# First norm of an encoder layer: statistics per token on tokens-major x, gain and split taken from PSUM, small loads behind the first weights

## What is computed

```python
def rmsnorm(x, g):
    xf = x.astype(jnp.float32)
    y = xf * lax.rsqrt(jnp.mean(xf * xf, axis=-1, keepdims=True) + EPS)
    return (y * g.astype(jnp.float32)).astype(x.dtype)

def hybrid_mixer(h, w_in, ...):          # h = rmsnorm(x, norm_mix)
    (qkv_a, a_pre, b_pre, z_a, q_b, k_b, v_b, i_b, f_b, o_b,
     q_c, k_c, v_c, gate_pre) = _split_cols(h @ w_in, IN_SIZES)
...
x = x + hybrid_mixer(rmsnorm(x, norm_mix[l]), w_in[l], ...)
```

## Time and profile before

| | |
|---|---|
| median of 3 runs | 2091.82 us (2091.56 to 2091.86) |
| the profiled execution | 2091.85 us |
| its span, first to last instruction | 2089.7 us |
| mean granted TensorE clock | 0.993 of full speed |
| busy: PE / DVE / ACT / POOL | 2045.9 / 1229.5 / 895.5 / 34.0 us |
| moved by DMA | 377.44 MB, 181 GB/s on average |

### The profile page before, as it was taken

How to read it: one execution, slowest core, us unless ns; L and a number is a source line. 1 busy time by engine, 2 the same in 40 slices (tenths; PEclk the granted TensorE clock), 3 DMA queues, 4 the chain that set the end, 5 groups by cost and what they waited for, 6 DMA issues and landing times.

```text
span 2089.7 us, 36639 instructions
## 1 busy us (share of the span) xinstructions
PE 2045.9 (98%) x15803; PEld 1974.7 (94%) x15803; DVE 1229.5 (59%) x1312; ACT 895.5 (43%) x864; POOL 34.0 (2%) x44
## 2 busy tenths in 40 slices
PE   5999999999999999999999999999999999999998
PEld 5999999999999999999999999888888888899998
DVE  5477644543544557577474445677877777744443
ACT  4444433344446434355444434544444444433332
POOL 2000000000000000000000000000000000000000
PEclk8999999999999999999999999999999999999999
DMA  7555444366455865655565355656655655566663
GB/s 220 162 184 185 137 135 133 109 207 198 150 177 176 297 203 177 226 162 181 182 196 167 122 160 171 223 173 199 193 179 190 201 181 180 180 202 198 185 195 126
DMA packets 358512, 377.44 MB, mean 181 GB/s; under 512 B 11913, under 2 KB 354723, under 8 KB 357123
## 3 DMA queue, kind: packets, MB, share of 16 engines
q1 hardware_dynamic: 354771, 353.36, 53.3%
q0 software_dynamic: 3632, 22.42, 2.9%
HBM read 364.75 MB, written 11.01 MB: 180 GB/s over the span
## 4 chain that ended last, share of the span: by engine, by line
PE 94%; DVE 3%; ACT 2%; issue 1%; DMA 0%; POOL 0%; SPq 0%; DVEq 0%; ACTq 0%
PE bank L1700 21%; PE bank L1702 21%; PE bank L1701 21%; PE bank L1734 15%; PE bank L1736 8%; PE bank L1911 1%; DVE w_lo L973 1%; PE bank L1858 1%; ACT w_hi L456 1%; PE bank L2114 1%; PE bank L2095 1%; DVE tmp L1017 1%; DVE x_home L1023 0%; PE bank L1845 0%; PE bank L1777 0%
## 5 line engine op out<-in xcount | busy, mean ns | idle before, releaser
L973 DVE TENSOR_TENSOR w_lo<-raw,w_hi 128x2048 fp32r<-128x2048 f32 (+1 forms) x352 | 763.6, 2169 | 624.4 <-ACT w_hi L456 624.0
L456 ACT ACTIVATE w_hi<-raw 128x2048 fp32r<-128x2048 f32 (+1 forms) x354 | 644.1, 1820 | 1098.7 <-PE bank L1702 823.8
L1700 PE MATMUL bank<-x_home,w_hi 128*128 128x256 f32 x2304 | 650.5, 282 | 18.8 <-DVE x_home L1023 15.4
L1701 PE MATMUL bank<-x_home,w_hi 128*128 128x256 f32 x2304 | 644.7, 280 | 0.0
L1702 PE MATMUL bank<-x_home,w_lo 128*128 128x256 f32 x2304 | 644.5, 280 | 0.0
L1734 PE MATMUL bank<-x_home,w_hi 128*128 128x512 f32 x1408 | 488.7, 390 | 3.6 <-DVE x_home L1582 2.2
L1700 PEld LDWEIGHTS bank<-x_home,w_hi 128*128 128x128 f32 x2304 | 434.9, 189 | 22.1 <-issue 13.7
L1701 PEld LDWEIGHTS bank<-x_home,w_hi 128*128 128x128 f32 x2304 | 434.9, 189 | 0.2
L1702 PEld LDWEIGHTS bank<-x_home,w_lo 128*128 128x128 f32 x2304 | 434.7, 189 | 0.0
L1736 PE MATMUL bank<-x_home,w_lo 128*128 128x256 f32 x1408 | 397.0, 282 | 0.0
L1734 PEld LDWEIGHTS bank<-x_home,w_hi 128*128 128x128 f32 x1408 | 264.3, 188 | 60.1 <-DVE xT L987 1.7
(11 more groups left out here) (279 smaller groups left out, 2181.0 us busy)
## 6 DMA issues: line engine op xcount, KB each, us to landing
raw<-in_w_in SPq DMA_DIRECT2D x53, 2048.0 KB, 8.6
raw<-in_ffn_up SPq DMA_DIRECT2D x44, 2048.0 KB, 8.1
raw<-in_ffn_down SPq DMA_DIRECT2D x32, 1408.0 KB, 6.5
raw<-in_xa_wkv SPq DMA_DIRECT2D x16, 2048.0 KB, 8.8
raw<-in_w_br SPq DMA_DIRECT2D x8, 2048.0 KB, 8.4
raw<-in_w_out SPq DMA_DIRECT2D x8, 2048.0 KB, 8.7
raw<-in_xa_wq SPq DMA_DIRECT2D x8, 2048.0 KB, 8.2
raw<-in_xa_wo SPq DMA_DIRECT2D x8, 2048.0 KB, 8.2
```

The costliest lines, as they stand in the source:

```text
L456: return nc.scalar.activation(out_, in_, func, **kw)
L973: tt(split_out(w_lo, kind, half), halves(raw, kind, half, par), split_out(w_hi, kind, half).bitcast(f32), ALU.subtract).then_inc(lo_ready, 1)
L1700: mm(o, w[0], x[0], start=start, stop=False)
L1701: mm(o, w[0], x[1], start=False, stop=False)
```

## The change

Only the start of the program changes.

- **SP**: the first half of x is issued first, then ident and the gain of this norm (norm_mix, with a semaphore of its own), the second half of x, unit 0 of the weights in two halves of its rows, unit 1. All other small loads follow: vectors, two gate loads instead of four (contiguous columns), masks and levels. Then comes unit 2, as before.
- **Statistics**: as each half of x lands, ScalarE (tokens 0 to 127) and VectorE (tokens 128 to 255) square it in place of the transposed copy and sum along the features in the same instruction. The statistics are two columns, x_rstd, instead of 128 x 256. The 32 matmuls with ones go.
- **Scaling**: x_tm is multiplied by x_rstd per token into x_n (in the space of conv, two instructions of 1024 elements on each of the two engines), and TensorE transposes x_n in 8 groups of 4 into banks 1 to 7 and 1 again. ScalarE takes the high part straight from PSUM with the gain as scale, VectorE the low part. xT is still made, for the residual.
- **Weights**: half 0 is split in two steps of eight blocks, before and between the upper parts. VectorE does the subtraction for halves 0 and 1. GpSimd does none, zeroes gw_hi and gw_lo instead of gw, and spills xT later, after half 4 is split (hi_ready 5).
- **Vectors**: the five transposes stand between halves 1 and 2; their copies and the gates' split, in four narrow instructions on each engine, follow on VectorE behind the subtraction for half 2.
- The semaphores' numbers in the later norms change with it (the first norm no longer counts).

The diff, cut to its core:

```diff
-            sp.dma_start(ident[:, :], c[:, 0:P]).then_inc(const_in, 16)
             for j in range(2):
                 sp.dma_start(x_tm[:, :, j * (D // 2):(j + 1) * (D // 2)], x_cols[:, :, j * (D // 2):(j + 1) * (D // 2)]).then_inc(x_in[j], 16)
+                if j == 0:
+                    sp.dma_start(ident[:, :], c[:, 0:P]).then_inc(const_in, 16)
+                    sp.dma_start(vecs[0:KC, 0, :], T["norm_mix"].rearrange("o (c p) -> (o c) p", p=P)).then_inc(mix_in, 16)
+            sp.dma_start(raw_0[:, 0:KC // 2, :], first_w[:, 0:KC // 2, :]).then_inc(w0_in, 16)
+            sp.dma_start(raw_0[:, KC // 2:KC, :], first_w[:, KC // 2:KC, :]).then_inc(raw_full[0], 16)
+            load(1, 0, W["w_in"][:, :, C_A + CW:C_A + 2 * CW], KC, first=True)
...
-            for m in range(2):
-                pool.wait_ge(hi_ready, m + 1)
-                pool.tensor_tensor(split_out(w_lo, FM, half), halves(raw, FM, half, par),
-                                   split_out(w_hi, FM, half).bitcast(f32), ALU.subtract).then_inc(lo_ready, 1)
+            pool.wait_ge(hi_ready, 5)
             pool.dma_start(x_spill, xT[:, :, :].rearrange("p c s -> p (c s)")).then_inc(spill, 16)
...
-            for c in range(4):
-                transposed(0, xT, c)
-                if c:
-                    squares(0, xT, c - 1)
-            squares(0, xT, 3)
-            root(0)
-            hi_half(*half_of(0))
-            act.wait_ge(set_up, 2)
-            for c in range(4):
-                upper_part(0, g_mix, x_hl, c)
-                if c == 1:
-                    hi_half(*half_of(1))
+            def x_squares(j):
+                act.wait_ge(x_in[j], 16)
+                copy(x_n[:, 0, j * (D // 2):(j + 1) * (D // 2)], x_tm[:, 0, j * (D // 2):(j + 1) * (D // 2)], ACT.Square,
+                     accum_out=x_sum[:, j, 0:1]).then_inc(xs_a, 1)
+            def first_upper(n):
+                act.wait_ge(xn_t, n + 1)
+                for x in range(2):
+                    last = copy(x_hl[:, 0, 2 * n + x, :], xb(n)[:, x * SEQ:(x + 1) * SEQ], scale=g_mix[:, 2 * n + x:2 * n + x + 1])
+                last.then_inc(xn_h, 1)
+            nc.scalar.preload_act_table_set("sqrt_and_others")
+            x_squares(0)
+            transposed(0, xT, 0)
+            transposed(0, xT, 1)
+            x_squares(1)
+            act.wait_ge(x_stat, 2)
+            copy(x_rstd, x_rstd, ACT.Sqrt).then_inc(x_root, 1)
+            transposed(0, xT, 2)
+            act.wait_ge(x_stat, 3)
+            x_scaled(0)
+            x_scaled(1)
+            transposed(0, xT, 3)
+            act.wait_ge(mix_e, 1)
+            first_weights(0, w0_h)
+            first_upper(0)
+            first_upper(1)
+            first_weights(1, hi_ready)
+            for n in range(2, 6):
+                first_upper(n)
+            hi_half(*half_of(1))
+            first_upper(6)
+            first_upper(7)
...
+                part = x_tm[:, 1, j * (D // 2):(j + 1) * (D // 2)]
+                v.scalar_tensor_tensor(x_n[:, 1, j * (D // 2):(j + 1) * (D // 2)], part, 1.0, part, ALU.mult, ALU.mult,
+                                       accum_out=x_sum[:, j, 1:2]).then_inc(xs_d, 1)
...
+            for n in range(8):
+                if n in (0, 4):
+                    pe.wait_ge(xn_a, n // 4 + 1)
+                    pe.wait_ge(xn_d, n // 4 + 1)
+                if n == 3:
+                    pe.wait_ge(tin_e, 4)
+                    pe.wait_ge(tin_d, 4)
+                if n == 7:
+                    pe.wait_ge(xn_l, 1)
+                for x in range(2):
+                    for a in range(TT):
+                        last = nc.tensor.transpose(xb(n)[:, x * SEQ + a * P:x * SEQ + (a + 1) * P],
+                                                   x_n[:, a, (2 * n + x) * P:(2 * n + x + 1) * P], ident[:, :])
+                last.then_inc(xn_t, 1)
+            for k in range(KC):
+                if k == 0:
+                    pe.wait_ge(w0_l, 1)
+                elif k == KC // 2:
+                    pe.wait_ge(lo_ready, 1)
+                if k % 2 == 0:
+                    pe.wait_ge(xn_l, k // 2 + 1)
+                w = [t[:, 0, k * P:(k + 1) * P] for t in (w_hi, w_lo)]
+                last = three(bank[0][:, 0:SEQ], w, [x_hl[:, j, k, :] for j in range(2)], k == 0, k == KC - 1)
```

More of the change, by code:

```diff
@@ L228, in build_program @@
         gqk = small[:, 100:104]
+        x_sum, x_rstd = small[:, 104:108].rearrange("p (j a) -> p j a", j=2), small[:, 108:110]
         g_mix, g_xa, g_mem, g_ffn = (vec1[:, 16 * i:16 * i + 16] for i in range(4))
@@ L344, in _ @@
             sp.dma_start(fb, T["ml_gate_bias"][0, 1:2, :].rearrange("o h -> h o")).then_inc(vec_in, 16)
-            load(0, 0, W["w_in"][:, :, C_A:C_A + CW], KC, first=True)
-            load(1, 0, W["w_in"][:, :, C_A + CW:C_A + 2 * CW], KC, first=True)
-            sp.wait_ge(gw_zero, 1)
-            for at, c0, k in ((0, C_AB, GH), (32, C_AB + GH, GH), (64, C_IF, MH), (96, C_IF + MH, MH)):
-                sp.dma_start(gw[:, :, at:at + k], W["w_in"][:, :, c0:c0 + k]).then_inc(gw_in, 16)
+            sp.dma_start(gw[:, :, 0:2 * GH], W["w_in"][:, :, C_AB:C_AB + 2 * GH]).then_inc(gw_in, 16)
+            sp.dma_start(gw[:, :, 2 * GH:2 * GH + 2 * MH], W["w_in"][:, :, C_IF:C_IF + 2 * MH]).then_inc(gw_in, 16)
+            sp.dma_start(upper[:, :], c[:, P:2 * P]).then_inc(causal_in, 16)
+            sp.dma_start(later[:, :], c[:, 2 * P:3 * P]).then_inc(causal_in, 16)
             sp.dma_start(lev[:, :, :], c[:, 3 * P:10 * P].rearrange("p (l n) -> p l n", l=7)).then_inc(lev_in, 16)
@@ L442, in mb, with xb @@
             return bank[4 + i % 4]
+        def xb(n):
+            return bank[1 + n % 7]
+        GATES = ((0, 0, GH), (32, GH, GH), (64, 2 * GH, MH), (96, 2 * GH + MH, MH))
         def up_bank(par, half):
@@ new lines, in first_upper, with first_weights @@
+            def first_upper(n):
[3 more added lines that the diff above has]
+                last.then_inc(xn_h, 1)
+            def first_weights(j, done):
+                act.wait_ge(*((raw_full[0], 16) if j else (w0_in, 16)))
+                ks = slice(j * (KC // 2), (j + 1) * (KC // 2))
+                copy(split_out(w_hi, FM, 0)[:, ks, :], halves(raw, FM, 0, 0)[:, ks, :]).then_inc(done, 1)
@@ L587, in _ @@
+            first_upper(0)
[6 more added lines that the diff above has]
+            first_upper(7)
+            beside(1)
+            act.wait_ge(gw_zero, 2)
+            act.wait_ge(gw_in, 32)
+            for at, c0, k in GATES:
+                last = copy(gw_hi[:, :, at:at + k], gw[:, :, c0:c0 + k])
+            last.then_inc(gw_h, 1)
             for m in range(2, 7):
@@ new lines, in first_weights @@
+            def first_weights(j, ready, done):
+                dve.wait_ge(ready, 1)
+                ks = slice(j * (KC // 2), (j + 1) * (KC // 2))
+                tt(split_out(w_lo, FM, 0)[:, ks, :], halves(raw, FM, 0, 0)[:, ks, :],
+                   split_out(w_hi, FM, 0)[:, ks, :].bitcast(f32), ALU.subtract).then_inc(done, 1)
+            v.memset(ones[:, :], 1.0).then_inc(set_up, 1)
+            x_squares(0)
+            transposed(0, xT, 0)
+            transposed(0, xT, 1)
+            x_squares(1)
@@ new lines, in _ @@
+            dve.wait_ge(xs_a, 2)
+            dve.wait_ge(xs_d, 2)
+            tt(x_rstd, x_sum[:, 0, :], x_sum[:, 1, :], ALU.add).then_inc(x_stat, 1)
+            dve.wait_ge(x_stat, 1)
+            v.tensor_scalar(x_rstd, x_rstd, 1.0 / D, EPS, ALU.mult, ALU.add).then_inc(x_stat, 1)
+            transposed(0, xT, 2)
+            dve.wait_ge(x_root, 1)
+            v.reciprocal(x_rstd, x_rstd).then_inc(x_stat, 1)
+            dve.wait_ge(x_stat, 3)
+            x_scaled(0)
+            x_scaled(1)
@@ new lines, in _ @@
+            transposed(0, xT, 3)
+            dve.wait_ge(mix_t, 1)
+            v.tensor_copy(g_mix, bank[0][:, 0:KC]).then_inc(mix_e, 1)
+            dve.wait_ge(mix_e, 1)
+            first_weights(0, w0_h, w0_l)
+            first_lower(0)
+            first_lower(1)
+            first_lower(2)
+            first_lower(3)
+            first_weights(1, hi_ready, lo_ready)
+            for n in range(4, 8):
+                first_lower(n)
+            lo_half(*half_of(1))
+            beside(1)
@@ L1087, in _ @@
+            last.then_inc(gw_l, 1)
             for m in range(2, 6):
@@ L1772, in transposes @@
                     last.then_inc(tin_t, 1)
-            def first_squares(c):
-                pe.wait_ge(n_sq, c + 1)
-                for j in range(4):
-                    last = mm(bank[3][:, 0:SEQ], ones[:, :], tmp[:, c % 2, j * SEQ:(j + 1) * SEQ], start=c + j == 0, stop=c + j == 6)
-                last.then_inc(n_ss, 1)
             def norm_beside(k, m, acts):
```

113 lines of the change are left out of this document (57 added, 56 removed).

## The result

| | before | changed |
|---|---|---|
| median | 2091.84 us (4 runs, 2091.56 to 2092.96) | **2076.1 us** (4 runs, 2075.57 to 2076.52) |
| profiled execution, its span | 2091.85, 2089.7 | 2076.52, 2074.7 |
| granted TensorE clock, mean | 0.993 | 0.996 |
| split of half 4 starts (the mark) | 56.68 | 41.54 |

The ratio is 0.992 with an interval of 0.9909 to 0.9932: 15.7 us, or 0.75%, faster. I had forecast 13.5 us less and 2078.3, with a range from 2075.9 to 2083.0.

The account below looks back on a forecast made before the run. TensorE, busy 98% of the span, bounds the kernel, so gains lie before its unbroken stream, in the first norm. The mark moves from 56.68 to 43.2, 13.5 us less: 2091.8 - 13.5 = 2078.3; range 2075.9 to 2083.0.

Parts of the forecast that it names:

- x lands: Start: x's first half, issued ahead of ident, comes 0.45 us earlier, landing at 7.3, first transpose at 7.45.
- Statistics: First norm: VectorE's second square and its sum end at 13.08; after root and inverse, scaling begins at 14.5.
- the first rival: VectorE's sum beside the square costs a second pass, 1.22 us instead of 0.19: 2079.3; 10%.
- Scaling to split: ScalarE works without a pause from 14.5 through scalings, splits and upper parts: 13.7 us, to 28.2.
- From the last upper part to half 1: VectorE ends its last lower pair at 29.0, then subtracts for half 1 in 2.29 us, to 31.3.
- TensorE: Matmuls: half 1 from 31.3 to 37.0, the vectors' transposes to 37.5, half 2 ends at 43.2, the mark.
- What is moved past queues: SP's reordered loads: SP free at 24 to 28; unit 2's load lands 39.4 to 45.9; lateness and later spill free.
- the low clock: Rival: TensorE's clock stays low through half 1, 5.1 us more: 2083.4; 8%.
- the time was not given back: Rival it denies: weights' stream or ScalarE's gate rows keep their own place in time, no gain: 2091.8; 2%.
- SP's queue starved nothing: Rival it denies: small loads in SP's queue delay later weights, 16 us slower, 2108; 2%.
- both rivals that widened it: Second pass for the sum (2079.3, 10%) and TensorE's low clock in half 1 (2083.4, 8%); whole range 2075.9 to 2083.0.

Follow-up runs that it names:

- Experiment 5: Changed kernel with one extra 1024-element copy on ScalarE between its scaling and the splits: mark less x's landing 35.23, 0.94 more; median 2076.7 us.
- experiment 2: Changed kernel with masks and small vector loads ahead of the weights again: mark less x's landing 34.28, no difference; median 2077.72 us.
- experiment 3: Changed kernel without GpSimd's wait for the split of half 4, so x is spilled early: mark less x's landing 34.29, no difference; median 2077.09 us.
- the second ones: Kernel before and changed kernel, unaltered, each profiled a second time: 2092.45 us (mark 56.85) and 2075.73 us (mark 41.18).
- experiment 8: Changed kernel with GpSimd subtracting half 1 and ScalarE splitting it behind the fourth upper part: mark less x's landing 32.90; median 2073.43 us.
- experiment 9: As experiment 8, with VectorE instead of ScalarE writing the first 1024 elements of w_hi: mark less x's landing 32.03; median 2073.8 us.
- experiment 6: Changed kernel with an extra 1024-element ScalarE copy while ScalarE waits for the sum of squares: mark less x's landing 34.30; median 2076.08 us.

## Why the prediction was right or wrong

The mechanism was right, and the gain came out at 15.1 instead of 13.5 us at the mark. The step that failed is a size: ScalarE's row from the scaling to the last upper part, put at 13.7 us and measured at 12.18. The points one by one:

- *x lands*: forecast 7.3, first transpose 7.45. Measured 7.25 and 7.45. Both numbers are right, the second by luck: I had the transpose follow x, and it waited for ident, which landed at 7.40.
- *Statistics*: the second square was to end at 13.08. Measured 12.98, where two small errors partly cancel. VectorE's second evacuation started at 11.15, not 10.98, and from its start to the end of the sum went 1.83 us, not 2.10:

```profile
11.76 1.22 DVE L1113 SCALAR_TENSOR_TENSOR conv<-proj 128x1024 f32<-128x1024 f32 x1
12.90 0.08 DVE L1113 DVE_READ_ACCUMULATOR conv<-proj 128x1 f32 x1
```

  The sum costs 0.08 us (I had 0.19) and no second pass, and the first rival is refuted. The Trainium skill's rule of half throughput ("Vector Engine (DVE) Microarchitecture Reference", section "Points that are easy to get wrong") does not hold for this form: with two float32 sources in SBUF and an accumulator it takes the same 1.22 us that 1024 elements take in the earlier trace rows. The small steps took 0.16 to 0.20 where I had 0.2, and VectorE's inverse hid behind ScalarE's evacuation, so the scaling began at 14.16, not 14.5: 0.34 us of the miss.
- *Scaling to split*: **this is the step that failed, a term that was mis-sized.** 13.7 us forecast, 12.18 measured (14.16 to 26.34), so it was put 1.52 us too long. ScalarE did the listed instructions in the listed order without a pause. But I added durations, and in an unbroken row the next instruction starts before the last has ended. The sixteen upper parts took 5.91 from start to start (1.42, 2.85, and 1.64 for the last four with the last one's end), not four times 1.70; the scalings 2.09 for 2.3; the evacuation 0.48 for 0.6; the two half splits 1.90 for 2.1; half 1's split 1.80 for 1.90. Experiment 5 shows the same on a single copy: it lasts 1.04 and costs 0.95. Overlap of that kind is about 1.0 of the 1.52. For the upper parts it was to be read from the earlier trace rows, where four of 1.70 are followed after 1.61, which makes 6.4 for sixteen. The other 0.5 is between that and the measured 5.91: upper parts now start every 0.36 us, where they started every 0.40. They now read PSUM instead of SBUF; whether that is the reason was not tried alone. I had kept 1 to 1.5 us for pieces that overlap as a bound, when it belonged in the middle. These 1.52 us and the 0.34 ahead of them make 1.86, of which the steps behind took back 0.2.
- From the last upper part to half 1: 3.1 forecast, 3.17 measured. Half 1's first matmul came at 29.57 at full clock, released by VectorE's w_lo, where I had 31.3.
- *TensorE*: 11.9 us from there to the mark forecast, 11.97 measured. The vectors' transposes run at 35.44, 5.87 behind half 1's start (forecast 5.7).
- *What is moved past queues*: SP free at 27.0 (forecast 24 to 28), unit 2's load issued at 29.69 behind half 1's subtraction. The loads and the spill are free (experiments 2 and 3). What I had wrong is where SP stands. I wrote that only element-wise gate loads are long, and it was the first small load behind the weights, a gain vector, that took 5.76 us; the next thirteen, a gate load among them, took 0.25 to 0.43 each, and three of the last four 1.51 to 2.50.
- *Rivals*: the low clock did not come (the Trainium skill, "TensorE: Matmul & The Clock Gate", section "HAM oscillation — how this bites in real kernels", has idle gaps bring it; here TensorE's waits of at most 2.18 us did not), the time was not given back (15.14 at half 4, 14.94 at half 326 in the profiled execution, with 16.74 between, from half 48), and SP's queue starved nothing.
- *The total*: the mark's gain is 15.14 between the first profiles and 15.67 between the second ones. The profiled executions differ by 15.33, and the medians by 15.7, because the changed kernel's median is 0.42 below its profiled execution; no profile shows where those other executions were faster.
- *The range*: my bounds below the forecast add up to 1.7 us (0.2 for the accumulator, 1.5 for overlap and small steps), which gives 2076.6. I wrote 2076.3, and then 2075.9 for the whole range, although both rivals that widened it make the kernel slower. So the 2076.1 lies inside the range by luck. At the mark the miss was 1.6 us, just within those bounds; nothing in them was for the clock behind the mark.

What stays open is which executions get the low clock at halves 28 and 48: the runs show the places, not the rule.

Experiments 8 and 9 beat both kernels by their marks: they are 1.4 and 2.3 us earlier than the changed kernel's. Their medians are 2.7 and 2.3 us below its 2076.1, and experiment 6, whose copy cost nothing at the mark and which was timed beside 8, had 2076.08. The intervals of the ratios overlap (0.9892 to 0.9925 for both, 0.9909 to 0.9932 for the changed kernel), so by the total the gain is likely and not shown.

## What to carry to other kernels

Cost an engine's unbroken row by the distance from one start to the next, not by adding durations: here the row took a tenth less than the durations added, and about two thirds of that was overlap. When an operation on VectorE is several times its usual length, look at what GpSimd reads at that moment, and change where the inputs lie before you take GpSimd's work away. For a change worth a few microseconds in a kernel of 2 ms, find an event just behind it and measure that: here the event repeated within 0.2 us, while the runs of one kernel spread over 0.7 to 4.7.

## What the runs showed of the hardware

- A VectorE instruction with two SBUF inputs that met GpSimd's subtraction (two SBUF inputs as well) was held for about its length: 5.52 us instead of 1.22 beside a subtraction of 5.52, 4.74 instead of 0.48 beside one of 4.78. VectorE instructions with one input in PSUM and one in SBUF were not (four in 1.66 us, with subtractions of 4.58 and 4.65 beside them).
- A sum of 1024 products along with scalar_tensor_tensor costs 0.08 us on VectorE; the same read costs 0.19 on ScalarE.
- The clock stayed at 2.4 GHz from 12 to 30 us although TensorE was busy for 0.64 of 2 us in one window and 0.90 in another, with waits of up to 2.18 us. Around half 48 one execution of the changed program was granted 0.63 of the clock over 4 us behind a thin stretch, another of the same program 1.00; that was worth 1.6 us.
- The issue of a small load mostly took 0.25 to 0.45 us. As the first behind 4 MB of weights on the same queue it took 5.76 (a gain vector) or 5.99 (a gate load), and loads further back were held at times too: 1.51 to 2.50 in the changed kernel, 5.71 in experiment 2, 5.62 in experiment 3.
